# Moving the four weight slots of an fp32r kernel to different places within 256 bytes

## What is computed

```python
for i in range(DEPTH):                       # DEPTH = 2
    h = rms_norm(x, norm_g[i])
    proj = h @ w_in[i]                       # 1024 x 9664: one projection feeds four branches
    y_a = (spatial_gating(...) * silu(a_z)) @ w_a_out[i]
    y_b = (multiscale_pool(...) * silu(b_z)) @ w_b_out[i]
    y_c = (latent_attention(...) * silu(c_z)) @ w_c_out[i]
    y_d = (stick_breaking_attention(...) * silu(d_z)) @ w_d_out[i]
    merged = sum(sigmoid(gates) * [y_a, y_b, y_c, y_d])
    x = x + merged @ w_o[i]
    x = x + sigmoid(rms_norm(x, ple_norm_g[i]) @ w_ple_gate[i]) * (p[i] @ w_ple[i])
```

## Time and profile before

| | us |
|---|---|
| median of 3 runs | 1371.41 |
| lowest and highest | 1370.64, 1374.18 |
| the profiled execution's own time | 1370.99 |
| its span, first to last instruction | 1369.2 |
| PE busy | 1361.3 (99%) |
| POOL busy | 554.7 (41%) |
| DVE, ACT busy | 692.8 (51%), 561.2 (41%) |
| DMA engines' mean share | 30% |

### The profile page before, as it was taken

One profiled execution on the slowest core, in us unless ns is written; L12 is line 12 of the kernel. 1 busy time (PEld: TensorE's weight loads), 2 busy tenths in 40 slices (PEclk: granted clock), 3 DMA queues, 4 the chain that ended last, 5 costly groups with the idle time before them and its releaser, 6 DMA issues.

```text
span 1369.2 us, 16133 instructions
## 1 busy us (share of the span) xinstructions
PE 1361.3 (99%) x6508; PEld 1148.5 (84%) x6508; DVE 692.8 (51%) x1051; ACT 561.2 (41%) x871; POOL 554.7 (41%) x233
## 2 busy tenths in 40 slices
PE   9999999999999999999999999999999999999998
PEld 8888888888888888888888888888888888888887
DVE  7966454155553323265767664451555532242743
ACT  6464463255552222224443644542555422222242
POOL 2334242534334444444454342424433444444443
PEclk9999999999999999999999999999999999999999
DMA  7322232322223333322343222222322233333332
GB/s 228 93 64 83 73 98 62 93 86 84 78 78 106 93 93 98 118 92 93 99 125 93 71 91 67 88 62 92 93 78 78 92 92 93 105 96 108 97 101 95
DMA packets 75354, 127.60 MB, mean 93 GB/s; under 512 B 8848, under 2 KB 45968, under 8 KB 75280
## 3 DMA queue, kind: packets, MB, share of 16 engines
q1 hardware_dynamic: 74048, 126.02, 30.0%
q10 hardware_dynamic: 1232, 0.55, 0.1%
HBM read 124.45 MB, written 2.10 MB: 92 GB/s over the span
## 4 chain that ended last, share of the span: by engine, by line
PE 94%; DVE 4%; ACT 1%; DMA 1%; issue 0%; POOL 0%; SPq 0%; ACTq 0%
PE ps L485 30%; PE ps L487 30%; PE ps L486 30%; PE ps L754 1%; PE ps L688 1%; PE ps L790 1%; PE ps L675 1%; DVE n_t L1459 1%; DVE h_lo L1316 0%; DVE ang L1375 0%; ACT w_hi L962 0%; DMA w_raw<-w_in 0%; PE ps L566 0%; DMA x<-x_in 0%; DVE xh L1485 0%
## 5 line engine op out<-in xcount | busy, mean ns | idle before, releaser
L460 POOL TENSOR_TENSOR w_lo<-w_raw,w_hi 128x1024 fp32r<-128x1024 f32 x222 | 548.1, 2473 | 771.3 <-ACT w_hi L962 771.2
L485 PE MATMUL ps<-h_hi,w_hi 128*128 128x512 f32 (+1 forms) x1096 | 427.3, 390 | 0.9 <-POOL w_lo L460 0.9
L487 PE MATMUL ps<-h_hi,w_lo 128*128 128x512 f32 (+1 forms) x1096 | 425.2, 388 | 0.0
L486 PE MATMUL ps<-h_lo,w_hi 128*128 128x512 f32 (+1 forms) x1096 | 425.0, 388 | 0.0
L962 ACT ACTIVATE w_hi<-w_raw 128x1024 fp32r<-128x1024 f32 x227 | 238.2, 1054 | 170.8 <-PE ps L487 166.1
L485 PEld LDWEIGHTS ps<-h_hi,w_hi 128*128 128x128 f32 x1096 | 205.9, 188 | 42.6 <-issue 1.2
L487 PEld LDWEIGHTS ps<-h_hi,w_lo 128*128 128x128 f32 x1096 | 205.8, 188 | 42.4
L486 PEld LDWEIGHTS ps<-h_lo,w_hi 128*128 128x128 f32 x1096 | 205.9, 188 | 41.1
L1760 DVE SCALAR_TENSOR_TENSOR m_part<-th,ps 128x512 f32<-128x512 f32 x48 | 33.0, 687 | 236.9 <-PE ps L487 236.8
L1180 ACT ACTIVATE th<-ps 128x512 f32<-128x512 f32 x48 | 28.7, 597 | 182.0 <-PE ps L487 182.0
L485 PE MATMUL ps<-act_hi,w_hi 128*128 128x512 f32 x192 | 75.2, 392 | 0.0
(11 more groups left out here) (334 smaller groups left out, 1970.7 us busy)
## 6 DMA issues: line engine op xcount, KB each, us to landing
w_raw<-w_in SPq DMA_DIRECT2D x172, 512.0 KB, 3.5
w_raw<-w_in SPq DMA_DIRECT2D x124, 128.0 KB, 2.5
w_raw<-w_in SPq DMA_DIRECT2D x36, 256.0 KB, 3.0
x<-x_in SPq DMA_DIRECT2D x8, 256.0 KB, 3.8
w_raw<-w_in SPq DMA_DIRECT2D x32, 64.0 KB, 2.1
out_x<-x SPq DMA_DIRECT2D x7, 256.0 KB, 3.8
rows<-rows_in SPq DMA_DIRECT2D x2, 768.0 KB, 5.3
p_raw<-p_in SPq DMA_DIRECT2D x2, 512.0 KB, 4.4
```

The costliest lines, as they stand in the source:

```text
L460: pool.tensor_tensor(w_lo_t[s][:], w_raw_t[s][:], w_hi_t[s][:].bitcast(F32), ALU.subtract).then_inc(w_lo_made, 1)
L485: pe.matmul(o, a_hi, b_hi, start=first, stop=False, skip_group_check=skip)
L486: pe.matmul(o, a_hi, b_lo, start=False, stop=False, skip_group_check=skip)
L487: return pe.matmul(o, a_lo, b_hi, start=False, stop=last, skip_group_check=skip)
```

## The change

Slot s of `w_raw` and `w_lo` begins at s * (4096 + 64) bytes from the first one instead of s * 4096. The first slot stays at byte 124800 (place 128). The others go to 128960 (place 192), 133120 (place 0) and 137280 (place 64). The arena begins 256 bytes later, at 141440, and keeps its place 128; so does each tensor in it. The four `w_hi`, `window` and all other tensors stay where they were. No instruction is added, removed or moved on any engine, no wait changes, and each DMA carries the same bytes in the same order; instructions differ in addresses alone.

```diff
-        ring_at = (nc.sbuf_base + 127) // 128 * 128
-        sb("arena", [P, (RING * CH + ARENA + 96) // 4])
-        arena_at = ring_at + RING * CH
+        SKEW = 64
+        ring_at = (nc.sbuf_base - P + 255) // 256 * 256 + P
+        sb("arena", [P, (RING * CH + 256 + ARENA + 256) // 4])
+        arena_at = ring_at + RING * CH + 256
...
-        w_raw_t = [at(f"w_raw{s}", s * CH, [P, 8, P], F32, ring_at) for s in range(RING)]
-        w_lo_t = [at(f"w_lo{s}", s * CH, [P, 8, P], F32R, ring_at) for s in range(RING)]
+        w_raw_t = [at(f"w_raw{s}", s * (CH + SKEW), [P, 8, P], F32, ring_at) for s in range(RING)]
+        w_lo_t = [at(f"w_lo{s}", s * (CH + SKEW), [P, 8, P], F32R, ring_at) for s in range(RING)]
```

## The result

The changed kernel takes 1389.11 us (median of 4 runs, 1388.15 to 1390.25) against 1371.12 us for the kernel before (4 runs): 18.0 us more, a ratio of 1.0131 with a 95% interval of 1.0119 to 1.0144. The forecast was no change, 1371.4 us, with a range up to 1376. It was wrong.

The account below looks back on a forecast made before the run. The prediction took PE's even matmul pace to bound the kernel. Its terms summed to 0 on the profiled execution's 1370.99 us; with the median of the runs shown 0.4 us above that, it forecast 1371.4 us, range 1367 to 1376.

Parts of the forecast that it names:

- What bounds the kernel: PE is busy 1361.3 of 1369.2 us; only the matmul pace or a late weight chunk can change the time.
- the terms for POOL, ACT and the DMAs: Subtractions, copies and loads on moved slots: each taken as 0, typically hidden by 6.7 us of slack; POOL under 3 us.
- the 0 for PE: 1396 matmuls with `w_lo` on moved slots: the operand's place does not change their pace, cost 0.
- the nearest row: `window` pieces at places 160 and 224 both take 0.34 us for three matmuls, so places show no effect.
- this hole: Caveat on the `window` evidence: its matmuls are short, and no loaded operand lies at another place than 128.
- The arithmetic of the columns: From 384 to 512 columns, 0.417 ns a column, one per clock: streaming without loss, plus a fixed 13.3 ns a matmul.
- The upper bound: PE on moved slots: the slower pace seen after a wait, 4.4 ns more for each of 1396 matmuls, +6.2 us.
- the sum: All parts of the change, from instructions to DMA, add up to 0 on the profiled execution's 1370.99 us.
- The rival on the slower side: Reads at places 64 and 192 need one more 128-byte fetch, slot 2 does not: 1375.5 to 1377.6 us, chance 0.08.
- The faster rival: Load and stream collide at place 128 as each matmul begins; the skew parts them: down to 1352.8 us, chance 0.06.
- The rule: From the Trainium skill: no dependence on the address within a partition is named, so a skew has nothing to relieve, 0.
- What would show it wrong: In the changed kernel: slot 0's chunks at another pace than the others, or all chunks' matmuls changing their pace.

Follow-up runs that it names:

- split_moved: The changed kernel with each weight chunk's product against `h` made in two goes, 384 then 128 columns: 1569.24 us; the kernel before, cut likewise, 1562.16 us.
- all64: Every tensor moved 64 bytes further on against the kernel before, all at place 192, relations kept: 1372.04 us, ratio 1.0002.
- map32: `w_hi` and `w_lo` of the four slots moved 32, 96, 160 and 224 bytes against the kernel before, activations unmoved: 1404.81 us, ratio 1.0244.
- hi_too: Both `w_hi` and `w_lo` of slot s moved 64 * s bytes against the kernel before, activations unmoved: 1391.87 us, ratio 1.0150.
- hi_alone: Only `w_hi` of slot s moved 64 * s bytes against the kernel before, `w_lo` left at place 128: 1395.43 us, ratio 1.0175.

## Why the prediction was wrong

- **What bounds the kernel** was right: PE's pace and nothing else, before and after. So were the terms for POOL, ACT and the DMAs in the steady stretches (2.40 us in the median, 1.05 us, landing in 3.4 us), the weight load of 188 ns, and slot 0 with 226.7 ns a matmul.
- **The step that failed** is the 0 for PE, "the nearest row", taken from `window`. Those matmuls have 16 to 144 columns. `split_moved` shows that a matmul of 128 columns doesn't feel the difference at all. In the changed kernel `window` runs as in the earlier trace rows, in 0.34 and 0.33 us for its three matmuls, between chunks that have slowed down:

```profile
85.39 0.27 PE L569 MATMUL ps<-window,bx_lo 128*128 128x144 f32 x1
...
85.73 0.27 PE L568 MATMUL ps<-window,bx_hi 128*128 128x128 f32 x1
...
86.62 0.27 PE L569 MATMUL ps<-window,bx_lo 128*128 128x144 f32 x1
...
86.95 0.27 PE L568 MATMUL ps<-window,bx_hi 128*128 128x128 f32 x1
```

  I had named this hole (short matmuls; no loaded operand at another place) and still gave the row 0.86 of the chance.
- **The arithmetic of the columns was right and answered another question.** From 384 to 512 columns the kernel before adds one column per clock, so the columns hold no loss that a skew could take away. The prediction read this as a sign that places don't matter. The trace held no long matmul with any other relation, so it said nothing on what another relation costs.
- **The upper bound** was 4.4 ns for each moved matmul, 6.2 us. Measured are 12 to 15 ns a loaded triple: up to 9 ns on one step, and the matmuls beside the moved one slow down as well. The border of the layers, 3.7 us in the profiled execution, has no term at all in the sum; the path from VectorE past POOL's subtractions to PE's `norm_sums` is not in it. With both, the loss is three times the bound.
- **The rival on the slower side** had the right sign and the wrong mechanism. It made slot 2 (place 0) harmless; slot 2 loses the most. Alignment as such is not it: `all64` is at place 192 throughout and loses nothing.
- **The faster rival**, a collision because everything begins at place 128, is refuted for 512 columns by `map32` and `hi_too`: every other relation is slower. Its idea that the fixed part of a matmul can shrink with the places is borne out with 256 columns: 120 ns less 256 columns at 0.417 ns are a fixed part of 13 ns, and at the difference 64 it is 7.
- **The rule** that contention in this memory is structural, by shared ports (the Trainium skill, SBUF — State Buffer, "SBUF: two separate sides", which also has TensorE wait on nobody, and whose 16-byte lines don't part these cases, as every operand here begins at a multiple of 32 bytes), does not cover this. TensorE's pace, 226.7 ns a matmul with one relation of the places and 233.4 ns with another, depends on addresses; the measurement decides.
- **What would show it wrong** was named rightly: "if every fourth chunk (slot 0) shows another pace than the three others". It does.

What stays open: why the relation matters, why it costs with 512 columns, hardly with 384, and gains with 256, and whether the matmul's own or the next one's loaded operand counts. No row shows the reads themselves. Whether the slower pace of nine matmuls after a wait has to do with it was not tested.

## What to carry to other kernels

Where TensorE is the bound with fp32r matmuls of 512 columns, begin both operands of all of them at the same place modulo 256 bytes, and treat an allocation that shifts one of them as a change of the kernel: here steps of 64 bytes cost 1.3%, and up to 2.4% was seen. Other types than fp32r were not tried. A row is evidence for a matmul only if it has the same length: the same difference lost 6 ns with 512 columns and gained 6 with 256. After a change of pace, look at the places where two engines just miss each other: they will not miss each other by the same distance again.

## What the runs showed of the hardware that I had not expected

- The pace of 512-column fp32r matmuls depends on the loaded operand's place minus the streamed one's, modulo 256 bytes: 227 ns at 0, about 229.5 at 192, 232.6 to 234.3 at the six others tried (steps of 32 bytes). Mixed differences cost more than the sum of their parts: (0, 0, 192) takes 694 ns a triple, (192, 192, 192) takes 689.
- The effect depends on the length, down to its sign: at the difference 64 a matmul takes 6 ns more with 512 columns, the same with 384 and 6 ns less with 256 (113.8 against 119.7).
- Stretches of 3.4 us at a granted clock of 0.50 came in several of the profiled executions. In the changed kernel one followed a wait of TensorE of 1.65 us. The wait alone does not decide it: `map32` waited 1.53 us at the same place (720.3 us) and kept 1.00, and in `hi_alone` a second stretch began at 781 us with no wait near it. What decides it is open.
- VectorE instructions of 0.7 us take 2.9 us when they meet GpSimd's subtraction; which of them do shifted here with the pace of a third engine.
